# Block 1's last expert pair as code of its own, with column halves through the scatter, the adds and the norm

## The reference

```
y = 0
for e in range(32):
    hid = silu(t @ w1[e]) * (t @ w3[e])          # 1024 -> 512
    y = y + comb[:, e:e+1] * (hid @ w2[e])       # 512 -> 1024; comb is 0 but for a token's two experts
h = h + ga2 * y
x = rmsnorm(h, g_final) * (1 + scf) + shf        # enters block 2's first FFN
...
return rmsnorm(x, final_norm_g)                  # end of block 2
```

## Time and profile before

| | us |
|---|---|
| median of 3 runs | 2258.42 (2256.83 to 2258.73) |
| span of the profiled execution | 2261.1 |
| PE busy | 2184.8 (97%) |
| DVE busy | 1240.1 (55%) |
| ACT busy | 426.6 (19%) |
| POOL busy | 50.5 (2%) |
| data moved | 499.98 MB, mean 221 GB/s |

### The profile page before, as it was taken

The page is one execution under the profiler, slowest core; times in us unless marked ns, Lnnn a source line. Parts: engine busy times, 40 slices in busy tenths (PEclk is TensorE's granted clock), DMA queues, the critical chain, the costliest instruction groups (busy, mean ns, idle before and its releaser), DMA issues.

```text
span 2261.1 us, 29957 instructions
## 1 busy us (share of the span) xinstructions
PE 2184.8 (97%) x12564; PEld 1481.3 (66%) x12564; DVE 1240.1 (55%) x2258; ACT 426.6 (19%) x858; POOL 50.5 (2%) x85
## 2 busy tenths in 40 slices
PE   7999999999999989999999999999999999999998
PEld 5778853433333337866968678856884976687873
DVE  2798422101110126676777766667666867767675
ACT  1123321101000012101142321101210132322110
POOL 1000100000000000000000000000000000000000
PEclk9999999999999999999999999999999999999999
DMA  9655587999999995444341435436453423245441
GB/s 406 266 223 232 223 277 303 421 421 421 422 421 421 421 390 161 163 168 167 113 163 45 149 122 174 162 130 214 159 181 135 168 83 125 78 151 182 159 181 42
DMA packets 174318, 499.98 MB, mean 221 GB/s; under 512 B 7128, under 2 KB 99560, under 8 KB 143984
## 3 DMA queue, kind: packets, MB, share of 16 engines
q1 hardware_dynamic: 169664, 481.23, 56.3%
q0 software_dynamic: 4384, 16.43, 2.2%
q10 hardware_dynamic: 144, 0.52, 0.1%
HBM read 491.34 MB, written 6.82 MB: 220 GB/s over the span
## 4 chain that ended last, share of the span: by engine, by line
PE 85%; DMA 9%; DVE 4%; ACT 1%; issue 1%; SPq 0%; POOL 0%; DVEq 0%; POOLq 0%
PE bank L2510 23%; PE bank L2558 11%; DMA ring<-in_w 8%; PE bank L1528 6%; PE bank L952 6%; PE bank L2623 6%; PE bank L1569 3%; PE bank L3053 2%; PE bank L2871 2%; PE bank L3126 2%; PE bank L1619 2%; PE bank L942 1%; PE bank L1056 1%; PE bank L1087 1%; PE bank L2602 1%; PE bank L1553 1%
## 5 line engine op out<-in xcount | busy, mean ns | idle before, releaser
L2510 PE MATMUL bank<-Tw,Sx 128*128 128x256 f32 x1032 | 229.9, 379 | 0.0
L2510 PEld LDWEIGHTS bank<-Tw,Sx 128*128 128x128 f32 x1032 | 193.0, 190 | 24.6
L1989 DVE TENSOR_TENSOR sg<-sg,bank 128x512 f32<-128x512 f32 x16 | 11.0, 688 | 283.4 <-PE bank L1528 283.4
L2510 PE MATMUL bank<-ring,xT 128*128 128x256 f32 x688 | 155.5, 379 | 0.0
L2510 PEld LDWEIGHTS bank<-ring,xT 128*128 128x128 f32 x688 | 130.5, 190 | 18.0 <-issue 0.5
L952 PE MATMUL bank<-xT,ring 128*128 128x256 f32 x640 | 141.8, 380 | 0.0
L952 PEld LDWEIGHTS bank<-xT,ring 128*128 128x128 f32 x640 | 120.7, 190 | 19.0 <-issue 3.3
L1528 PE MATMUL bank<-ring,xg 128*64 128x512 f32 x512 | 114.5, 594 | 18.5 <-DMA ring<-in_w 18.5
L1569 PE MATMUL bank<-ring,hTg 128*64 128x512 f32 x512 | 113.4, 595 | 0.0
L3550 DVE TENSOR_TENSOR whole<-bank,part 128x256 f32<-128x256 f32 (+1 forms) x133 | 57.5, 432 | 99.5 <-PE bank L2510 98.4
L2558 PE MATMUL bank<-Tw,Sx 128*128 128x512 f32 x240 | 108.9, 592 | 0.0
(11 more groups left out here) (643 smaller groups left out, 3761.6 us busy)
## 6 DMA issues: line engine op xcount, KB each, us to landing
ring<-in_w SPq DMA_DIRECT2D x128, 1024.0 KB, 23.9
ring<-in_ffn_w_in SPq DMA_DIRECT2D x88, 1024.0 KB, 7.7
ring<-in_first_pieces SPq DMA_DIRECT2D x33, 2048.0 KB, 11.9
more<-in_w SPq DMA_DIRECT2D x48, 1024.0 KB, 23.6
ring<-in_ffn_w_out SPq DMA_DIRECT2D x20, 2048.0 KB, 7.8
ring<-in_w_mix_in SPq DMA_DIRECT2D x12, 2048.0 KB, 7.9
ring<-in_xattn_w_kv SPq DMA_DIRECT2D x5, 2048.0 KB, 7.9
spare<-in_w SPq DMA_DIRECT2D x8, 1024.0 KB, 26.3
```

What stands on the lines that cost most here:

```text
L2510: last = nc.tensor.matmul(bank[BANK_OF[name]][:, 0:SEQ], lhs(k), rhs(k), start=(k == 0), stop=(k == 3))
```

## The change

For the last pair alone (i = 7, q = 1), PE makes no gather; ACT and DVE take none. Its down product (`last_down`) goes by column halves: all of half 0 into bank 0, then all of half 1 into bank 1, each counted up on its own; both waits for the weights (`moe_full[4]` and `moe_full[5]`) stand ahead of it. DVE multiplies each half by `ga2` as soon as it is there. The scatter of the last pair (`last_scatter`) uses all 128 rows in one matmul for each half and tile, and DVE adds each bank to `x` when its matmul is done. DVE's loop has one iteration less, and the last two pairs are written out; `final_gain` moves ahead of the last `ye`. Four fillers follow instead of six.

The norm at the end of block 1: ACT squares by halves and tiles, scaled so that the sums are means. DVE multiplies half 0 by the gain, adds the two partial means (`mean_of_halves`, a 128x2 instruction), and waits for POOL, which only takes the power. DVE then writes half 0 of `x`, multiplies half 1 by the gain, and writes half 1. The last norm of block 2 takes the sum of halves on DVE too. Three semaphores are merged or renamed (`routed`, `part_down`).

```diff
+            def last_down(n):
+                pe.wait_ge(hT_ready, n + 1)
+                for c in range(2):
+                    pe.wait_ge(moe_full[4 + c], n * 32 + 32)
+                for half in range(2):
+                    for c in range(4):
+                        for e in range(2):
+                            last = nc.tensor.matmul(bank[half][e * CAP:(e + 1) * CAP, :], ...)
+                        if (half, c) == (0, 3):
+                            last.then_inc(part_down, 1)
+                        elif half and c % 2:
+                            last.then_inc(hid_down, 1)
+            def last_scatter():
+                for half in range(2):
+                    pe.wait_ge(ye_dve, 2 * PAIRS + half + 1)
+                    for t in range(NT):
+                        nc.tensor.matmul(bank[4 + 2 * t + half][:, :], whotT[:, 1, t * P:(t + 1) * P],
+                                         ye[:, half, :], start=False, stop=True).then_inc(scattered, 1)
...
-                        if q == 1:
+                        last_pair = hi == PAIRS // 2 and q == 1
+                        if q == 1 and not last_pair:
                             gather(i + 1, 0, (0, 1))
                         scatter((q + 1) % 2, 0, 2 * n + 1)
                         turn(i, q)
                         scatter((q + 1) % 2, 1, 2 * n + 2)
+                        if last_pair:
+                            last_down(n)
+                            continue
...
-            pe.wait_ge(ye_dve, 2 * PAIRS + 2)
-            for turn_ in range(2):
-                scatter((PAIRS + 1) % 2, turn_, 2 * PAIRS + turn_ + 1, stop=turn_ == 1)
-            for _ in range(6):
+            pe.wait_ge(scattered, 2 * PAIRS + 1)
+            last_scatter()
+            for _ in range(4):
...
-            for t in range(NT):
-                last = nc.scalar.activation(xs[:, t, :], x[:, t, :], ACT.Square, accum_out=ss[:, t:t + 1])
+            for half in range(2):
+                for t in range(NT):
+                    last = nc.scalar.activation(xs[:, t, cs], x[:, t, cs], ACT.Square, scale=ROOT,
+                                                accum_out=ss[:, 2 * half + t:2 * half + t + 1])
...
             for half in range(2):
                 for t in range(NT):
                     st(nc.vector.tensor_tensor(y[:, t, cs], x[:, t, cs], scf_row[:, cs], ALU.mult))
-            st.sync()
-            dve.wait_ge(rstd_ready, N_FINAL + 1)
-            for half in range(2):
+                if half == 0:
+                    mean_of_halves(dve, N_FINAL)
+                    dve.wait_ge(rstd_ready, N_FINAL + 1)
+                st.sync()
                 for t in range(NT):
                     ins = nc.vector.scalar_tensor_tensor(out=x[:, t, cs], in0=y[:, t, cs], ...)
...
+            hidden(PAIRS - 1)
             final_gain(dve, st)
+            dve.wait_ge(part_down, 1)
+            weighted_out(0)
+            dve.wait_ge(hid_down, 2 * PAIRS)
+            weighted_out(1)
+            for half in range(2):
+                for t in range(NT):
+                    dve.wait_ge(scattered, 2 * PAIRS + 1 + 2 * half + t + 1)
+                    add_experts(dve, half, t, bank[4 + 2 * t + half][:, :])
...
+        def mean_of_halves(dve, n):
+            dve.wait_ge(ss_ready, n + 1)
+            nc.vector.scalar_tensor_tensor(out=ms[:, 0:NT], in0=ss[:, 0:NT], scalar=EPS, in1=ss[:, NT:2 * NT],
+                                           op0=ALU.add, op1=ALU.add).then_inc(ms_ready, 1)
+        def rstd_of_halves(pool, n):
+            pool.wait_ge(ms_ready, n + 1)
+            pool.sem_inc(pool_passed, 1)
             nc.gpsimd.tensor_tensor(rstd[:, 0:NT], ms[:, 0:NT], neghalf[:, 0:NT], ALU.pow).then_inc(rstd_ready, 1)
```

More of the change, by code:

```diff
@@ L19 @@
 EPS = 1e-6
+ROOT = D ** -0.5
 CAP = 64
@@ L1575, in down @@
                         last.then_inc(hid_down, 1)
+            def last_down(n):
[5 more added lines that the diff above has]
+                        for e in range(2):
+                            last = nc.tensor.matmul(bank[half][e * CAP:(e + 1) * CAP, :],
+                                                    hTg[:, c * P + e * CAP:c * P + (e + 1) * CAP],
+                                                    down_rows(8 + 2 * (c // 2) + e)[:, c % 2,
+                                                                                    half * 512:(half + 1) * 512],
+                                                    start=(c == 0), stop=(c == 3))
+                        if (half, c) == (0, 3):
[8 more added lines that the diff above has]
+                                         ye[:, half, :], start=False, stop=True).then_inc(scattered, 1)
             gather(0, 0, (0, 1))
@@ L1677, in down @@
                                     last.then_inc(hid_down, 1)
-                    last.then_inc(hid_down if e else dense_down, 1)
+                    last.then_inc(hid_down if e else part_down, 1)
                 for g in range(4):
@@ L1856, in vector_moe @@
                     st.sync(back=1)
-                    nc.vector.tensor_scalar(fits[:, :], most[:, :], TCAP + 0.5, None, ALU.is_lt).then_inc(fits_ready, 1)
+                    nc.vector.tensor_scalar(fits[:, :], most[:, :], TCAP + 0.5, None, ALU.is_lt).then_inc(routed, 1)
                 st.sync()
@@ L1979, in vector_gathered, with hidden, weighted_out @@
             gathered(0, 1, 3)
-            for i in st.loop(PAIRS // 2, 2):
+            def hidden(n):
+                dve.wait_ge(moe_silu, n + 1)
+                dve.wait_ge(hid_up, n * 4 + 4)
+                nc.vector.tensor_tensor(sg[:, 1, :], sg[:, 0, :], bank[3][:, :], ALU.mult).then_inc(h_ready, 1)
+            def weighted_out(half):
+                nc.vector.tensor_tensor(ye[:, half, :], bank[half][:, :],
+                                        ga2_row[:, half * 512:(half + 1) * 512], ALU.mult).then_inc(ye_dve, 1)
+            for i in st.loop(PAIRS // 2 - 1, 2):
                 for q in range(2):
@@ L1997, in vector_gathered @@
                     for half in range(2):
-                        nc.vector.tensor_tensor(ye[:, half, :], bank[half][:, :],
-                                                ga2_row[:, half * 512:(half + 1) * 512], ALU.mult).then_inc(ye_dve, 1)
-            final_gain(dve, st)
[L2001 to L2011, removed]
+                        weighted_out(half)
+            hidden(PAIRS - 2)
+            dve.wait_ge(hid_down, 2 * PAIRS - 2)
+            for half in range(2):
+                weighted_out(half)
+            hidden(PAIRS - 1)
+            final_gain(dve, st)
+            dve.wait_ge(part_down, 1)
+            weighted_out(0)
+            dve.wait_ge(hid_down, 2 * PAIRS)
+            weighted_out(1)
+            for half in range(2):
+                for t in range(NT):
+                    dve.wait_ge(scattered, 2 * PAIRS + 1 + 2 * half + t + 1)
+                    add_experts(dve, half, t, bank[4 + 2 * t + half][:, :])
         def vector_dense(dve, st):
@@ L2052, in vector_dense @@
                 st(nc.vector.tensor_tensor(xs[:, t, :], xs[:, t, :], ga2_row, ALU.mult))
-                add_experts(dve, st, t)
+            st.sync()
+            for half in range(2):
+                for t in range(NT):
+                    add_experts(dve, half, t, xs[:, t, half * 512:(half + 1) * 512])
         FB, N_DOWN = NGRP, (NGRP + 1) // 2
```

63 lines of the change are left out of this document (32 added, 31 removed).

## The result

The changed kernel is slower: 2266.18 us in the median of six runs (2259.17 to 2266.75) against 2258.27 for the kernel before in the same rounds, a ratio of 1.0028 (95% interval 1.0017 to 1.0038). Ratios here are taken over all runs and can differ a little from the quotient of the medians. In a second set of rounds (experiment 1) it was 2264.66 against 2258.99 (11 and 29 runs), 1.0023 (1.0014 to 1.0032). I had forecast 2259.0 and at most 2261.2, with 0.93 on no measurable change. By the medians the loss is 5.7 to 7.9 us.

The account below looks back on a forecast made before the run. Weights bound the experts' stage and PE bounds from 848 us; the change works on 818 to 848 us. -0.55 + 1.3 - 0.2 = +0.55 us on 2258.42 gave 2259.0 us, range 2256.2 to 2261.2.

Parts of the forecast that it names:

- the wait for the last weights: Ahead of the last down product: PE idles 3.45 us and starts at 828.15, later by 1.41 than before.
- the clock at the down product: Last down product: the clock falls after the idle stretch, costing 0.85 to 1.7 us, taken as 1.3.
- the pipelined end and the norm: End of block 1: last add 1.06 us earlier; last add to last write 6.7 us instead of 6.2, power 0.71.
- At no cost: Renamed semaphores, the third FFN piece's later wait, the moved `final_gain` and two fillers less were said to cost nothing.
- the rival of two falls: Block 2's first transposes: the clock falls there too, 1.3 us more (at most 1.7), 2260.3 us; chance 0.12.
- one fall, not two: Main case: the clock falls only while the last down product runs, 2259.0 us; chance 0.5.
- the forecast path: Last pair through block 1's norm: second half's transposes start at 846.14 instead of 846.69, gaining 0.55 us at unchanged clock.
- the last norm's -0.2: Last norm of block 2: the power ends at 2255.27 instead of 2255.49, a gain of 0.2 us.

Follow-up runs that it names:

- experiment 1: The changed kernel run and profiled once more, against the kernel before: 2264.66 us, ratio 1.0023.
- experiment 5: The changed kernel, its last down product taking row chunks 0 and 1 of both halves before the wait for the last weights: 2259.75 us, ratio 1.0003.
- experiment 17: The changed kernel with two fillers instead of four behind the scatter: 2265.91 us, ratio 1.0022.
- experiment 3: Only the norms' part of the change, with the last pair done as in the kernel before: 2259.41 us, ratio 0.9999.
- experiment 2: Only the pair's part of the change, with the norm ending block 1 done as in the kernel before: 2265.51 us, ratio 1.0022.
- experiment 10: The changed kernel with the last weights' wait behind row chunks 0 and 1, two fillers and sixteen 16-column matmuls behind the scatter: 2259.17 us, ratio 0.9997.
- experiment 9: The changed kernel with the last weights' wait behind row chunks 0 and 1, three 16-column matmuls ahead of down, three behind the fillers: 2256.30 us, ratio 0.9986.
- experiment 15: The changed kernel with the last weights' wait behind row chunks 0 and 1 and six 16-column matmuls ahead of the down product: 2258.22 us, ratio 0.9992.
- experiment 16: The kernel of experiment 15 with two fillers added between the halves of block 2's first transposes: 2255.75 us, ratio 0.9980.
- experiment 7: The changed kernel with three full fillers ahead of the early wait and three 16-column matmuls behind the four fillers: 2260.22 us, ratio 1.0003.
- 4: The changed kernel with six fillers instead of four, and two between the halves of block 2's first transposes: 2265.26 us, ratio 1.0029.
- 12: The changed kernel, early wait kept, with three 16-column matmuls ahead of the down product: 2266.11 us, ratio 1.0035.
- 14: The changed kernel, last weights' wait behind row chunks 0 and 1, three 16-column matmuls ahead of down, six fillers, two between transpose halves: 2264.39 us, ratio 1.0019.
- experiment 6: The changed kernel with six 16-column matmuls behind the four fillers: 2262.89 us, ratio 1.0014.
- 8: The changed kernel with the last weights' wait behind row chunks 0 and 1 and six 16-column matmuls behind the fillers: 2259.14 us, ratio 0.9998.
- 11: The changed kernel with the last weights' wait behind row chunks 0 and 1, two fillers and twelve 16-column matmuls behind the scatter: 2260.12 us, ratio 1.0001.

## Why the prediction was wrong

**Right: the wait for the last weights.** Down began 0.13 us behind the landing, PE idle for 3.37 us; I had 828.15 and 3.45. Without the early wait (experiment 5) the distance to the kernel before goes from 5.7 to 0.5 us; 5.2 less, of which 3.5 would be the half product that no longer stands behind the landing and 1.6 the clock.

**Right in kind, short in size: the clock at the down product.** I took 1.3; experiment 1 shows 8.68 - 7.09 = 1.6. Of the seven profiles of kernels with the early wait and an idle PE ahead of it, six have the fall; the changed kernel's first profile is the seventh. By the rule of the Trainium skill's "TensorE: Matmul & The Clock Gate" (What's actually happening) an idle array goes back to half rate; these six agree. The seventh does not show it, and experiment 17 paid more than I had called the most, 1.7: its product took 9.68, which is 2.6 us.

**Right: the pipelined end and the norm.** The last add ended 11.6 us behind the landing (forecast 11.3), the power took 0.71 with VectorE standing, and from the last add to the last write it was 838.43 - 831.69 = 6.7 us, as forecast. The norms alone changed nothing (experiment 3).

**Wrong: "At no cost".** This was the step that failed. I wrote that two fillers less cost nothing but idle time, and looked at the code's place only in the rival of two falls, as a thing that would have to happen besides. Two costs that the sum put at nothing were paid, about equal in experiment 1: the stop, 2.2 us, and the second fall of the clock, 2.4 us. The stop comes with the pair's part of the change (experiment 2 has it, 3 has not). It stands between the transposes, behind the last wait for x, where each us of it counts; before, the same eight transposes ran in 1.09. The change takes 56 PE instructions away ahead of the branch that ends the experts, and the stop slides with such instructions. But experiment 10 puts 56 back and has a stop of 4.4 us, so their number alone doesn't say why the kernel before had none. That stays open.

**Wrong: one fall, not two.** I gave the second fall 0.12. It is in the first profile and in that of experiment 1, and in both it begins during the transposes, ahead of the stop; in the first profile the stop begins at 839.18, and the window just ahead of it is at half clock:

```profile
838.75:839.15 0.40, 0.40 (x3) 0.25 (x2) 0.40 (x2) 0.00 (x0) 0.40 (x1) 0.50 1.02 335
```

Experiments 9 and 15 have the fall with no stop at all, and experiment 16 shows the clock kept with the second gap filled. The length of the two gaps around the first eight transposes doesn't decide alone: experiment 3 has gaps of 1.23 and 1.69 us, behind six fillers, and experiment 7 has 0.82 and 1.60, and both kept the clock. Windows over the transposes, experiment 9 and then 3:

```profile
835.80:842.60 6.80, 5.82 (x13) 3.45 (x14) 5.37 (x11) 2.91 (x6) 2.17 (x3) 0.50 1.10 354
```

```profile
841.00:849.00 8.00, 5.09 (x24) 2.93 (x23) 7.19 (x12) 3.51 (x7) 1.17 (x2) 1.00 1.08 341
```

The sum by experiment 1, from the landing (824.58) to the end of the transposes (848.49), is 23.9 us; before it was 846.69 + 1.09 - 828.1 = 19.7. That is 4.2 more: the forecast path -0.2 (18.4 against 18.6), the slow down product 1.6, the stop 2.2, and transposes at half clock 0.7 (rounded). The first products then run at half clock until 851.9, 3.4 x 0.5 = 1.7. With the last norm's -0.2 it is 5.7 us, and the medians differ by 5.67. That this agrees so closely is luck in part: the profile is of a run 3.3 us above its kernel's median, and the span of the trace before alone lies 2.7 above its own.

**What the stop is.** Shown is that it stands at a fixed place in PE's code and slides with the instructions ahead of it, over seven kernels and once foretold. That code is loaded at this place is not shown directly, since the page lists the instruction queue's transfers but not for which engine each is. Their times fit, though. In the kernel before, two transfers of 16 KB start 0.45 us apart where the branch is passed, and both have landed 3.2 us ahead of the first transposes; in the changed kernel one starts there (832.2), and the second only at 838.5, when the second half of x has arrived. DMA windows: 837 to 842 us before, then 838 to 839 us after.

```profile
q8 instruction: 2, 0.03, 4.6%
```

```profile
q8 instruction: 1, 0.02, 7.2%
```

The same transfers in other traces, in us from the span's start:

| kernel | stop behind transpose | first transfer starts | second transfer | PE goes on |
|---|---|---|---|---|
| 17 | 15 | 840.5 | 846.8 to 848.0 | 849.3 |
| changed | 11 | 832.2 | 838.5 to 839.6 | 841.1 |
| 4 | 7 | 834.7 | 840.3 to 841.4 | 842.6 |
| 12 | 5 | 836.9 | 843.3 to 844.5 | 845.9 |
| 14 | 1 | 833.7 | 840.1 to 841.2 | 842.6 |
| 10 | ahead of the first | 833.7 | 838.8 to 840.0 | 841.5 |
| 6 | ahead of the first | 842.5 to 843.6 | none ahead of the stop's end | 845.1 |

In all 13 profiles with the stop PE goes on 1.2 to 1.5 us behind the end of such a transfer. And where it lies between the transposes, it ends 7.9 to 9.1 us behind the start of the first transfer, wherever it begins. So a few instructions more or less move the stop's beginning and set its length (0.7 to 4.9 us), but not its end.

The Trainium skill has the rule, in "Runtime: NRT & Kernel Launch" (Instruction fetch mechanics): code is streamed in blocks of 256 instructions, and a taken branch whose target isn't at hand must wait for its block. It calls the crossing of a block's end mostly hidden; if the stop is such a crossing, it was not hidden behind this branch, with 0.7 to 4.9 us. I had not looked there. Experiments 7, 9, 15 and 16 have a second transfer too, 5.2 to 6.3 us behind the first, and no stop. My expectation for 15 had said that there would be no second load; if theory D holds, it is there, but PE doesn't need that code yet. Experiments 6 and 8 have as many instructions as 7. In the first two the matmuls ahead of the branch end just when x arrives, and the transfer starts only then (842.49 in experiment 6), so the branch's own load shows as 2.6 us; in experiment 7 it starts 1.8 us before those matmuls end. That, and the 4.4 us of experiments 10 and 11, which have two transfers 5.1 and 4.3 us apart, is argued and not isolated. Why the second transfer comes so soon after the first in the kernel before, and so late in the changed one, no run shows.

## What to carry to other kernels

Before a matmul group is moved forward, take the landing of its last operand from the trace even if nothing waits for it now; here a wait moved ahead of the product ate the whole gain of the removed work, and splitting the product at the landing (experiment 5) took the loss against the kernel before from 5.7 to 0.5 us. When a change adds or removes instructions ahead of a branch, look at PE's "issue" time behind the branch in the new profile; if there is a stop, slide it with a few cheap instructions to see whether it hangs on the code's place, and look at the instruction queue's transfers beside it. Sliding it ahead of the first transpose did not hide it here (2.6 to 4.4 us); what removed it was adding 24 instructions with at least half of them ahead of the down product, and adding the same 24 behind the fillers did not. Fill thin stretches around a hand-over as well as empty ones, but only where the filling itself can't be late: in experiments 4 and 14 it ran behind a stop and cost time. Measure each with the clock row of a window.

## What the runs showed of the hardware

A stop of PE with nothing to wait for, of up to 4.9 us, whose place moved one transpose for every two instructions added, in both directions, and which ended 1.2 to 1.5 us behind a 16 KB transfer of the instruction queue in all 13 profiles that have it. TensorE's clock fell in a stretch where PE did transposes with gaps of 1.3 and 1.7 us (experiment 15), and it did not when the second gap was filled by two matmuls (experiment 16); the kernel before survived gaps of 2.27 and 0.36 around the same transposes, and experiment 3 gaps of 1.23 and 1.69. POOL's power took 0.71 us in block 1's norm and in the last one wherever VectorE stood waiting for it, against up to 1.68 beside a working VectorE, and its first instruction after 200 us of rest was no slower.
